# Attention of a hybrid encoder layer on one Trainium2 core: local and full heads in turn, the full heads' values products moved into the next tile, loops unrolled, and turns read under a float32r name

## The reference

```python
h = rmsnorm(x, g_attn); qa, ka, va, qb, kb, vb = jnp.split(h @ w_in, splits, axis=-1)
# A: blocks of 128 queries against 384 keys, |q - k| <= 128, with a bias and a sink
s = jnp.einsum('bqhgd,bkhd->bhgqk', qb, kb) * scale + bias
m = jnp.maximum(jnp.max(s, axis=-1, keepdims=True), sink_f); e = jnp.exp(s - m)
p = e / (jnp.sum(e, axis=-1, keepdims=True) + jnp.exp(sink_f - m))
oa = jnp.einsum('bhgqk,bkhd->bqhgd', p, vb)
# B: blocks of 128 queries against all T keys, normed q and k with rotary positions
s = jnp.einsum('bqhgd,bkhd->bhgqk', qb, k) * scale
ob = jnp.einsum('bhgqk,bkhd->bqhgd', jax.nn.softmax(s, axis=-1), v)
x = x + concat(rmsnorm(oa, g_out_a), rmsnorm(ob, g_out_b)) @ w_out
x = x + expert_choice_moe(rmsnorm(x, g_ffn), ...)        # 16 experts
x = x + sigmoid(rmsnorm(x, g_ple) @ w_ple_gate) * (p @ w_ple_proj); y = rmsnorm(x, g_final)
```

## Time and profile before

| | us |
|---|---|
| median of 3 runs (1643.95 to 1644.47) | 1644.11 |
| the profiled execution | 1646.54 |
| its span, first to last instruction | 1644.8 |
| PE busy, share of the span | 1476.2, 90% |
| DVE busy | 933.9, 57% |
| ACT busy | 724.2, 44% |

### The profile page before, as it was taken

One profiled execution on the slowest core, in us unless ns is written; L12 is line 12 of the kernel. 1 busy time (PEld: TensorE's weight loads), 2 busy tenths in 40 slices (PEclk: granted clock), 3 DMA queues, 4 the chain that ended last, 5 costly groups with the idle time before them and its releaser, 6 DMA issues. The chain is left out here.

```text
span 1644.8 us, 21515 instructions
## 1 busy us (share of the span) xinstructions
PE 1476.2 (90%) x7320; PEld 1035.4 (63%) x7320; DVE 933.9 (57%) x1325; ACT 724.2 (44%) x1157; POOL 183.0 (11%) x249
## 2 busy tenths in 40 slices
PE   5999996599999959869998969999999999948997
PEld 4777775465566635548887746666566666627885
DVE  5444443477667747722238856667677676643553
ACT  4333333466666637712222443454454444423332
POOL 1111111000000000010000211112112112021110
PEclk9999998799999979979999979999999999978998
DMA  7433322622111053153442746878878878753331
GB/s 253 92 109 108 108 96 105 227 75 102 67 62 54 13 194 124 53 193 126 150 153 77 246 163 210 267 262 256 270 248 263 260 255 264 242 169 123 121 137 64
DMA packets 118848, 261.53 MB, mean 159 GB/s; under 512 B 7649, under 2 KB 37473, under 8 KB 115721
## 3 DMA queue, kind: packets, MB, share of 16 engines
q1 hardware_dynamic: 110592, 233.55, 40.3%
q0 software_dynamic: 7168, 25.17, 6.5%
q10 hardware_dynamic: 1032, 2.10, 1.1%
HBM read 194.20 MB, written 66.58 MB: 159 GB/s over the span
## 5 line engine op out<-in xcount | busy, mean ns | idle before, releaser
L1734 DVE TENSOR_TENSOR moe_w_lo<-ring,moe_w_hi 128x2048 fp32r<-128x2048 f32 x96 | 220.4, 2296 | 165.2 <-ACT moe_w_hi L1673 165.0
L1673 ACT ACTIVATE moe_w_hi<-ring 128x2048 fp32r<-128x2048 f32 x96 | 183.6, 1914 | 204.4 <-PE moe_p_g L1853 77.6
L1408 PE MATMUL mix_p_big<-kept_out_w,mix_m_hi 128*128 128x512 f32 x384 | 125.6, 409 | 4.4 <-DVE mix_m_lo L1283 2.5
L504 PE MATMUL proj_p_out<-proj_w_hi,proj_h_hi 128*128 128x512 f32 x264 | 110.8, 420 | 9.6 <-DVE proj_q_hl L400 9.6
L1861 PE MATMUL moe_p_gu<-ring,moe_xT_r 128*64 128x512 f32 x512 | 116.9, 598 | 0.0
L504 PE MATMUL proj_p_out<-proj_w_hi,proj_h_lo 128*128 128x512 f32 x264 | 105.0, 398 | 0.0
L504 PE MATMUL proj_p_out<-proj_w_lo,proj_h_hi 128*128 128x512 f32 x264 | 104.9, 397 | 0.0
L957 DVE TENSOR_REDUCE sample_ntop<-sample_p_s 128x1 f32<-128x1024 f32 x64 | 78.3, 1224 | 44.0 <-PE sample_p_s L779 43.8
L793 PE MATMUL sample_p_t<-sample_ident,sample_probs 128*128 128x128 f32 x688 | 99.6, 277 | 3.8 <-ACT sample_probs L895 2.5
L793 PEld LDWEIGHTS sample_p_t<-sample_ident,sample_probs 128*128 128x128 f32 x688 | 81.2, 142 | 20.1 <-ACT sample_probs L895 5.6
L1408 PEld LDWEIGHTS mix_p_big<-kept_out_w,mix_m_hi 128*128 128x128 f32 x384 | 72.4, 194 | 21.3 <-DVE mix_m_lo L1283 2.9
(11 more groups left out here) (293 smaller groups left out, 3155.6 us busy)
## 6 DMA issues: line engine op xcount, KB each, us to landing
ring<-in_w_gate SPq DMA_DIRECT2D x32, 1024.0 KB, 5.7
ring<-in_w_up SPq DMA_DIRECT2D x32, 1024.0 KB, 7.6
ring<-in_w_down SPq DMA_DIRECT2D x32, 1024.0 KB, 7.3
qT_d<-proj_qT SPq DMA_DIRECT2D x12, 1024.0 KB, 3.9
sample_q<-qT_d SPq DMA_DIRECT2D x8, 1024.0 KB, 5.3
proj_x<-in_x SPq DMA_DIRECT2D x12, 512.0 KB, 4.2
proj_w_raw<-in_w_in SPq DMA_DIRECT2D x8, 768.0 KB, 5.9
kT_d<-proj_kT SPq DMA_DIRECT2D x12, 512.0 KB, 3.6
```

Of the source, the lines that this page charges most:

```text
L504: last = pe.matmul(p_out[:, cols], h[:, s, k, :], w[:, k, cols], start=(k == 0 and n == 0), stop=(k == KC - 1 and n == 2))
L1408: mm = pe.matmul(p_out[:, cols], m[:, s, k, :], ww[:, k, cols], start=(k == 0 and n == 0), stop=(k == KC - 1 and n == 2))
L1673: act.activation(w_hi[:, at % SPLIT], raw[:, at % RAW], ACT.Copy).then_inc(hi_made, 1)
L1734: dve.tensor_tensor(w_lo[:, at % SPLIT], raw[:, at % RAW], w_hi[:, at % SPLIT].bitcast(F32), ALU.subtract).then_inc(lo_made, 1)
```

## The change

It does five things.

1. Order of heads: A and B alternate (0, 8, 1, 9, ...), but in the first tile of each call four A heads come first and four B heads last. A turn comes three steps after its scores (`LAG = 3`), not two. A heads have one bank of scores (`p_sa`), B heads two (`p_sb`).
2. Values products: A's are made at once (three blocks) in step 2 of the next tile, B's two blocks at a time (one for prompt) in steps 7, 8, 10 and 11. Both, and the turns of their results, share the one bank `p_o`. `pT_b` gets a second buffer. `turn_o` comes in steps 4 and 13, `rows` in 5 and 14.
3. Everything in `attend` is unrolled, with no loop.
4. All turns read float32r: `sb_both` gives a tile a second name of that type, and `make_identity` makes the float32r identity with one more copy on POOL.
5. The maximum of an A head comes straight from the custom operation (sign turned, sink as its start), without the small operation behind it. Bias and sinks are loaded from ACT's queue, q in halves, and the parts of `w_out` are split in steps 8 and 12 of every prompt tile.

```diff
+    early = [0, 1, 2, 3, 8, 4, 9, 5, 10, 6, 11, 7, 12, 13, 14, 15]
+    order = [(u, head) for u in range(n) for head in (early if u == 0 else even)]
+    PV_B = {7: (0, n // 4), 8: (n // 4, n // 2), 10: (n // 2, 3 * n // 4), 11: (3 * n // 4, n)}
...
+            def turn(g):
+                u, head = order[g]
+                lo, hi = edges(u) if head < HEADS else (0, 4)
+                pe.wait_ge(exp_done, g + 1)
+                for r in range(rounds[g]):
+                    m = first_round[g] + r
+                    if m >= 2:
+                        pe.wait_ge(t_out[m % 2], m // 2)
+                    for b in range(lo, hi):
+                        at = (4 * r + b) * P
+                        mm = pe.transpose(p_t[:, m % 2, b, :].bitcast(F32R), probs_r[:, g % 4, at:at + P], ident_r[:])
+                    mm.then_inc(t_done, 1)
...
+            for g in range(END + LAG):                      # PE
+                u, j = divmod(g, STEPS)
+                if g < END:
+                    scores(g)
+                if g >= LAG:
+                    turn(g - LAG)
+                if 1 <= u < n:
+                    if j == 2:
+                        values_a(u - 1)
+                    if j == 4:
+                        turn_o(u - 1, A)
+                    if j in PV_B:
+                        values_b(u - 1, *PV_B[j])
+                    if j == 13:
+                        turn_o(u - 1, B)
...
+            for g in range(END + LAG):                      # ACT
+                u, j = divmod(g, STEPS)
+                if g >= LAG:
+                    copy_turned(act, 0, g - LAG, copy)
+                if g < END:
+                    exponentials(g)
+                    if next_chunk(u, j) is not None:
+                        w.high(act, next_chunk(u, j))
+                if 1 <= u < n:
+                    if j == 1:
+                        sink(u - 1)
+                    if j == 3:
+                        out_of_psum(u - 1, A)
+                    if j == 6:
+                        square(u - 1, A)
+                    if j == 12:
+                        out_of_psum(u - 1, B)
+                    if j == 15:
+                        square(u - 1, B)
...
+            for g in range(END + LAG):                      # DVE
+                u, j = divmod(g, STEPS)
+                if g < END:
+                    maximum(g)
+                    if j and next_chunk(u, j - 1) is not None:
+                        w.low(dve, next_chunk(u, j - 1))
+                if g >= LAG:
+                    copy_turned(dve, 1, g - LAG, copy)
+                if 1 <= u < n:
+                    if j == 0:
+                        sink(u - 1)
+                        if u >= 2:
+                            mean_of(u - 2, B)
...
+                    if j == 14:
+                        rows(u - 1, B)
...
-                    mm = pe.transpose(p_mT[:, k, :], m_sb[:, s, k * P:(k + 1) * P], ident[:])
+                    mm = pe.transpose(p_mT[:, k, :].bitcast(F32R), m_r[:, s, k * P:(k + 1) * P], ident_r[:])
```

More of the change, by code:

```diff
@@ L641, in attend, with p_out, next_chunk @@
         block = ctx.enter_context(nc.Block())
[L643 to L668, removed]
-            if not begun:
-                tile(0, 0, True, False)
-            with engine.Fori(0, (n - 2) // 2) as m:
-                tile(m * 2 + 1, 1, False, False)
-                tile(m * 2 + 2, 0, False, False)
-            tile(n - 1, 1, False, True)
+        def p_out(u, g):
+            return p_o[:] if u < n - 1 or g == A else p_sb[:, 0, 0:BANK].rearrange("p (h q) -> p h q", h=GROUP)
+        def next_chunk(u, j):
+            return 2 * u + (8, 12).index(j) if w and j in (8, 12) else None
         @block.sync
@@ L777, in scores @@
[L777 to L790 removed]
+                    if g != at_a[0]:
+                        pe.wait_ge(ntop_done, at_a[at_a.index(g) - 1] + 1)
@@ new lines, in scores @@
+                    out, keys, spans = p_sa, ka[:, s], [slice(lo * P, hi * P)]
+                else:
+                    b = at_b.index(g)
+                    if b >= 2:
+                        pe.wait_ge(exp_done, at_b[b - 2] + 1)
+                    out, keys, spans = p_sb[:, b % 2], kb, [slice(c, c + BANK) for c in range(0, T, BANK)]
+                for cols in spans:
+                    for part in range(2):
+                        made = pe.matmul(out[:, cols], q_sb[:, s, head, :], keys[:, 2 * kv + part, cols],
+                                         start=(part == 0), stop=(part == 1))
@@ L853, in _ @@
-            pe.wait_ge(ident_ready, 1)
-            run(pe, tile)
-            for head in (14, 15):
-                turn(n - 1, head, False, False, True)
-            for j in range(3, HEADS):
-                values_b(n - 1, j)
-            turn_o_b(n - 1)
-        def copy_turned(eng, bank, i, s, head, first, last, fresh, copy):
-            kv, g = head % HEADS // GROUP, head % GROUP
-            for r in range(rounds(head)):
-                n_round = round_of(0, head, r)
-                if n_round % 2 != bank:
+            pe.wait_ge(ident_ready, 1)
@@ L867, in copy_turned @@
+            values_a(n - 1)
+            values_b(n - 1, 0, n)
+            turn_o(n - 1, A)
+            turn_o(n - 1, B)
+        def copy_turned(eng, bank, g, copy):
+            u, head = order[g]
+            lo, hi = edges(u)
+            kv, h = head % HEADS // GROUP, head % GROUP
+            for r in range(rounds[g]):
+                m = first_round[g] + r
+                if m % 2 != bank:
                     continue
-                eng.wait_ge(t_done, i * per_tile + n_round + 1)
+                eng.wait_ge(t_done, m + 1)
@@ L869, in copy_turned @@
                 if head < HEADS:
[L870 to L877 removed]
+                    if u:
+                        eng.wait_ge(pv_done[A], u)
@@ L891, in exponentials @@
                 if head < HEADS:
[L892 to L899 removed]
+                    cols = slice(lo * P, hi * P)
```

548 lines of the change are left out of this document (251 added, 297 removed).

## The result

The changed kernel takes 1666.97 us (median, 1666.05 to 1668.96) against 1644.29 of the kernel before beside it: ratio 1.0138, interval 1.0120 to 1.0155. It is slower by 22.7 us, outside the forecast range. Of these the profiled executions show 20.1 (spans of 1664.9 and 1644.8), because the one of before lies 2.4 above its median.

A forecast was written before the change was run, and what follows sets the result against it. PE was taken to pace every stage the change touches. The terms -10 + 0.3 + 9 + 0.5 + 1.7 + 1 = +2.5 gave 1646.5 us on the median of 1644.1 (+0.15%), with a range of 1628 to 1661.

The forecast's parts named there:

- The walk of the steps: Sample tile's 16 steps walked in the new order: waits 6.5, less 0.5 overlap, a tile of 36.7 us against 35.2.
- Point 1: Sample step 4: PE waits 1.8 us to turn A's result, its copy on ACT standing behind step 3's exponential.
- Point 2: Sample steps 6 and 10: PE waits 0.9 us each for bank 1's copy, on DVE behind a full head's maximum.
- Point 3: Sample steps 1 and 2: PE waits 2.2 us; DVE's mean awaits ACT's square in step 0, making copies late.
- Point 4: Sample step 13: PE waits 0.7 us to turn B's result, behind the exponential of step 12.
- The tile of before: Sample tile before the change: 33.0 us by step prices against 35.2 measured, the 2.2 between read as waits.
- The clock falls: Rival, chance 0.07: idling PE drops partly to 1.2 GHz, +3 us a sample tile, +2 a prompt tile, 1675 in all.
- the term of the tiles: Seven sample tiles at +1.5 us each, less 1.5 for first and last: +9, bounds -32 and +21.
- The first tile: Start of sample: earlier overlap lost because the first full head waits for keys, +0.5 us, ends -3 and +4.
- The turns: Float32r name outside attention: 0.16 us saved on eight turns, -10 in all, bounds 0 and -12.
- The last tile: End of sample, behind the last scores: local values blocks ahead of B's and both normalisations behind, +1.7 us (0 to 3).
- prompt: Prompt's 4 tiles: PE's work falls 1.3 a tile, waits rise slightly more; +1 us, from -7 to +7.

The follow-up runs named there:

- e10: Changed kernel with ACT copying results out of PSUM first in steps 3 and 12, and all local heads' copies on ACT in sample: 1625.4 us, 0.9880.
- e2: Changed kernel with the turns in both attention stages back to float32: 1666.8 us, 1.0134 of the kernel before.
- e5: Changed kernel with PE making local heads' scores twice in tiles 1 to 7 of sample, as filler: 1664.6 us, 1.0110.
- e8: Changed kernel with six float32r turns of q ahead of each local head's scores in tiles 1 to 7 of sample: 1666.1 us, 1.0124.
- e6: Changed kernel with bias and sinks issued by SP behind the first q and ka, not from ACT's queue: 1659.6 us, 1.0075.
- e1: Attention of the kernel before (order, loops, loads), with all turns under the float32r name, the rest as changed: 1624.9 us, 0.9881.
- e7: e10 with bias and sinks issued first by SP, and mean and scaling of B's rows moved to steps 1 and 3: 1624.8 us, 0.9875.
- e9: e7 with the turns in both attention stages back to float32: 1628.9 us, 0.9898 of the kernel before.
- e11: e10 with bias and sinks issued first by SP, mean of B's rows left in step 0: 1622.7 us, 0.9853.
- e4: Changed kernel with ACT copying every round of local heads in sample, DVE keeping bank 1 of full heads: 1649.3 us, 1.0027.

## Why the prediction was wrong

- **The walk of the steps held.** Tile 36.66 against 36.7. Point 1: 1.71 for 1.8. Point 2: 0.86 and 0.85 for 0.9 each. Point 3: 1.47 for 2.2. Point 4: 0.56 for 0.7. Taking the two copies away in e10 takes most of the waits away. The reason given for point 3 holds too, by the rows of DVE above. That the tile came out to 0.1 us is partly luck: the waits were 5.45 for 6.0 and PE's own work 31.2 for 30.7. The tile of before was misread in the same way: 33.0 of work and 2.2 of waits, where the earlier trace rows has 34.4 and 1.5.
- **The step that failed is the clock.** The sum priced all of PE's work at 2.4 GHz, while it forecast 6 us of idling in a tile that had idled 1.5. The rival *The clock falls* had 0.07 of the chance, and its price was too high (+3 a tile; it was 0.6 to 2.2). The dips are nearly all of the 12 us by which the term of the tiles is short: e2, in the same order and without a dip, takes 262.5 from the first scores of tile 1 to the last full head's; less 1.3 in each of seven tiles that is 253.4, an estimate of the changed kernel without dips. It is 9.7 above before, where the forecast was 9, and 11.3 under the 264.7 measured. In e5 and e8, where PE is given work and nothing else, the clock is back. The forecast also counted turns as a third of PE's instructions; in a sample tile of before they are half of them, at clock 1.00.
- **The first tile was mis-sized**, +5.0 for +0.5, outside its ends of -3 and +4. The argument looked at the first full head and its keys, and that head's scores (315.69) do not wait for keys. What is late first is the maximum of the first local head: the bias shares the DMA engines with all that SP issues at that time and lands 6 us later. e6 shows it. The Trainium skill (DMA: Bandwidth & Descriptors, Issuing engines are not separate DMA queues), quoted in the forecast for no gain, says that such transfers interleave; here that made a loss, since the load that is needed first no longer came first.
- **The turns were right**: 10.3 for 8 behind attention (7.2 to 12.5 over all runs with that code). In the projection PE's timeline has the saving:

```profile
236.25 0.40 PE L510 MATMUL proj_p_out<-proj_w_hi,proj_h_lo 128*128 128x512 f32 x1
236.50 0.80 PE L483 MATMUL proj_p_xT<-proj_ident_r,proj_xn_r 128*128 128x128 f32 x8
...
237.44 0.40 PE L510 MATMUL proj_p_out<-proj_w_lo,proj_h_hi 128*128 128x512 f32 x1
```

  1.19 from product to product, where 1.33 stood. The stage is no shorter in this execution, since PE waits 4.5 us for ACT's qT in it, and 2.9 before. In e10, with the same projection, that wait is 2.4, and the stage ends at 290.4, 2.1 earlier than before, for 1.9 forecast. What moves the wait from run to run is open.
- **Inside attention** the name gives 1.3 to 1.6 us a tile in three pairs (before and e1, e7 and e9, the changed tile at full clock and e2).
- **The last tile** (+1.5 for +1.7) was right, **prompt** was +2.9 for +1, with its clock at 0.83 against 0.91. That the clock is the reason is not shown: e10's prompt takes 116.3 at 0.82.

## What to carry to other kernels

An order that hands work to another engine "in time" should be walked by queue: here three copies stood behind an exponential or a maximum, and taking them from behind it, with one load put first, turned a kernel 1.4% slower than before into one 1.5% faster (e11). Of that, the new name alone gives 1.2% (e1), and it needed no new order: test the parts of a change apart. When a change shortens PE's work and adds waits, price the clock too: read it per tile, and test with filler work in the waits. A load that is needed first should be issued ahead of the large ones (e6); on another engine's queue it shared the DMA engines here and landed 6.2 us later.

## What the runs showed of the hardware

- With six more turns in eight steps of a tile (e8) the granted clock was 1.00 throughout, where it was 0.91 to 0.96 without: turns held it as well as products (e5).
- Longer turns (88 in a tile, PE busy for 2.2 us more, the tile 1.3 longer) kept the clock at 1.00 with the waits left in place, 4.6 us for 5.45 (e2 against the changed kernel). What exactly decides is open: e4 dips with less idle time than e2.
- In a tile the time at the lower level, 3 to 7 us (twice what the mean clock lacks of 1.00, times the tile), cost 0.6 to 2.2 us: 1.7 where some 3 fell on values products, 0.6 where they fell ahead of a wait, and 2.1 to 2.2 for 7.
